# A two-layer diffusion trunk on one core: the FFN's closing norm and residual move into the FFN's program, and the modulation weights are loaded ahead of x

## What is computed

```
mod = split(silu(c) @ ada_w[layer] + ada_b[layer], 6)            # for the latent tokens; c_ctx for the context
h   = rms_norm(x, norm_pre_mix) * (1 + mod[1]) + mod[0]          # then four groups of mixing heads, and w_out
x   = x + mod[2] * rms_norm(o, norm_post_mix)
f   = conv_ffn(rms_norm(x, norm_pre_ffn) * (1 + mod[4]) + mod[3], w_up, conv, w_down)
x   = x + mod[5] * rms_norm(f, norm_post_ffn)                    # the closing norm and residual
rms_norm(v, g) = v * rsqrt(mean(v * v over the 1024 features) + 1e-6) * g
```

## Time and profile before

| What | us |
|---|---|
| median of three runs (4760.15 to 4768.19) | 4762.68 |
| the profiled execution's own time | 4763.57 |
| its span, first to last instruction | 4760.6 |
| TensorE busy in the span | 3919.5 (82%) |
| VectorE / ScalarE / GpSimd busy | 2133.6 / 1343.8 / 1150.1 |
| mean granted TensorE clock, share of full | 0.907 |

### The profile page before, as it was taken

One profiled execution on the slowest core, in us unless ns is written; L12 is line 12 of the kernel. 1 busy time (PEld: TensorE's weight loads), 2 busy tenths in 40 slices (PEclk: granted clock), 3 DMA queues, 4 the chain that ended last, 5 costly groups with the idle time before them and its releaser, 6 DMA issues. The chain is left out here.

```text
span 4760.6 us, 81723 instructions
## 1 busy us (share of the span) xinstructions
PE 3919.5 (82%) x33438; PEld 3150.5 (66%) x33438; DVE 2133.6 (45%) x2920; ACT 1343.8 (28%) x1879; POOL 1150.1 (24%) x884
## 2 busy tenths in 40 slices
PE   5999559576878999999993999559658888999995
PEld 2888435364767788888882787435437767888884
DVE  3444735465556432332236323735465555332234
ACT  4111333234333321211213211333243334222221
POOL 1000520203531232332321000520205512333322
PEclk8999669797988999999996999669779989999997
DMA  4444110101012111101101234110110021111112
GB/s 164 161 158 157 46 61 0 39 3 35 4 53 85 54 36 38 39 31 40 40 27 62 105 128 142 42 58 1 39 36 4 4 101 59 49 49 44 48 49 88
DMA packets 71558, 283.24 MB, mean 59 GB/s; under 512 B 7392, under 2 KB 12768, under 8 KB 66272
## 3 DMA queue, kind: packets, MB, share of 16 engines
q1 hardware_dynamic: 55136, 198.51, 12.2%
q10 hardware_dynamic: 16128, 80.49, 4.6%
HBM read 223.65 MB, written 47.45 MB: 57 GB/s over the span
## 5 line engine op out<-in xcount | busy, mean ns | idle before, releaser
L3444 DVE SCALAR_TENSOR_TENSOR y<-ps,taps,y 128x1023 f32<-128x1023 f32 (+1 forms) x132 | 134.2, 1016 | 866.2 <-DVEq L3442 859.7
L491 PE MATMUL ps<-h_hi,wu_hi 128*128 128x512 f32 x1680 | 460.4, 372 | 12.3 <-PEq L3344 12.3
L491 PE MATMUL ps<-h_hi,wu_raw_rest 128*128 128x512 f32 x1680 | 459.4, 371 | 0.0
L491 PE MATMUL ps<-h_whole_rest,wu_hi 128*128 128x512 f32 x1680 | 459.0, 371 | 0.0
L3489 POOL TENSOR_TENSOR wu_raw_rest<-wu_raw,wu_hi 128x1024 fp32r<-128x1024 f32 x84 | 201.3, 2397 | 1025.8 <-POOLq L3488 1025.8
L491 PE MATMUL ps<-h_hi,w_hi 128*128 128x512 f32 (+1 forms) x1200 | 314.9, 367 | 39.6 <-PEq L487 39.6
L491 PEld LDWEIGHTS ps<-h_hi,wu_hi 128*128 128x128 f32 x1680 | 294.6, 188 | 69.6 <-issue 13.5
L491 PEld LDWEIGHTS ps<-h_hi,wu_raw_rest 128*128 128x128 f32 x1680 | 294.6, 188 | 56.3
L491 PEld LDWEIGHTS ps<-h_whole_rest,wu_hi 128*128 128x128 f32 x1680 | 294.1, 188 | 56.2
L491 PE MATMUL ps<-h_hi,w_raw_rest 128*128 128x512 f32 (+1 forms) x1200 | 313.1, 365 | 0.0
L491 PE MATMUL ps<-h_whole_rest,w_hi 128*128 128x512 f32 (+1 forms) x1200 | 313.0, 365 | 0.0
(11 more groups left out here) (390 smaller groups left out, 8141.4 us busy)
## 6 DMA issues: line engine op xcount, KB each, us to landing
wu_raw<-in_w_up_dram SPq DMA_DIRECT2D x88, 512.0 KB, 3.3
w_raw<-in_w_in_dram SPq DMA_DIRECT2D x54, 512.0 KB, 4.6
ada_w<-in_ada_rest_dram ACTq DMA_DIRECT2D x27, 1024.0 KB, 6.8
rows<-rows ACTq DMA_DIRECT2D x42, 640.0 KB, 4.9
wd_raw<-in_w_down_dram SPq DMA_DIRECT2D x40, 512.0 KB, 4.2
h_whole<-rows SPq DMA_DIRECT2D x24, 640.0 KB, 6.3
ada_w<-in_ada_rest_dram ACTq DMA_DIRECT2D x27, 512.0 KB, 4.8
raw<-rows SPq DMA_DIRECT2D x20, 640.0 KB, 4.7
```

What stands on the lines that cost most here:

```text
L491: mm = pe.matmul(ps[:, lo:lo + width], w[a][:, t, :], rhs[b][:, t, lo:lo + width], start=(t == 0 and i == 0), stop=(t == n_k - 1 and i == 2))
L3444: dve.scalar_tensor_tensor(y[:, s, lo + 1:hi], ps[s][:, lo:hi - 1], k.taps[:, s, 0:1], y[:, s, lo + 1:hi], ALU.mult, ALU.add).then_inc(own ...
```

## The change

It has three places.

1. **Start.** `load_phase` loads only tiles 0 and 1 of x. The other six are issued by SyncE in the next block, behind its four tiles of modulation weights and ahead of the projection weights. TensorE multiplies seven tiles of modulation weights ahead of the ones product, and one after. VectorE's `between()` (the rests of the two projection weights) comes ahead of its wait for the turned sums.
2. **Closing inside the FFN's program, both layers.** `residual_phase` is gone. The spilled x comes back tile by tile into `k.h`, behind the last down weights. In the last group ScalarE squares each output tile when it is complete and multiplies it in place by its modulation (ACT.Identity with a scale), and VectorE adds the squares into `facc` between its additions. One ones product of `facc` and Ln and Exp follow. VectorE then multiplies each tile by the factor and adds x; the x of tiles 1, 3 and 5 is added by GpSimd.
3. **What follows a closed tile.** In layer 0 ScalarE squares it, TensorE sums it over features at once (ones products accumulated over the eight tiles), and the factor of layer 1's first norm is ready at the block's end in `k.factor`; layer 1's `Norm` begins with `between()` and the scaling. In layer 1 each closed tile is stored by a DMA of its own, and `store_phase` is gone.

The core of the diff:

```diff
@@ load_phase, Norm.sync
-                for t in range(KD):
+                for t in range(2):
                     sp.dma_start(k.xT[:, t, :], a["xT"][:, t, :]).then_inc(k.x_tiles[t].sem, 16)
...
             self.load_ada(sp, 0)
+            for t in range(2, KD):
+                sp.dma_start(self.k.xT[:, t, :], self.x[:, t, :]).then_inc(self.k.x_tiles[t].sem, 16)
@@ Norm.scalar, Norm.vector: squares, sum and factor only `if self.ada is not None`; in vector also
+        between()
         if self.ada is not None:
             dve.wait_ge(self.turned.sem, self.turned.at(1))
...
-        between()
-        dve.wait_ge(self.root_dve, 1)
-        dve.sem_inc(self.root_dve, -1)
+            dve.wait_ge(self.root_dve, 1)
+            dve.sem_inc(self.root_dve, -1)
@@ Norm.tensor
-            self.ada_products(pe, 0, KD // 2)
+            self.ada_products(pe, 0, KD - 1)
...
-            self.ada_products(pe, KD // 2, KD)
+            self.ada_products(pe, KD - 1, KD)
@@ input_projection_phase
-                norm.tensor(pe)
+                if layer == 0:
+                    norm.tensor(pe)
@@ mix_out_ffn_phase, SyncE behind load_last_down(sp)
+        def close_layer(sp):
+            for t in tiles:
+                sp.dma_start(k.h[:, t, 0:n], k.x_dram[:, t, 0:n]).then_inc(x_back.sem, 16)
+            if layer == DEPTH - 1:
+                for t in tiles:
+                    wait_closed(sp, t)
+                    sp.dma_start(a["out"][:, t, :], k.xT[:, t, 0:SEQ]).then_inc(stored.sem, 16)
+                sp.wait_ge(stored.sem, stored.at(16 * KD))
@@ VectorE: in vector_down's last group behind the addition of tile o: add_square(dve, o - 1)
+        def add_square(dve, o):
+            if o < 1:
+                return
+            dve.wait_ge(fsq_done.sem, fsq_done.at(o + 1))
+            if o > 1:
+                dve.wait_ge(facc_done.sem, facc_done.at(o - 1))
+            dve.tensor_tensor(facc, facc, y[:, o % 2, 0:n], ALU.add).then_inc(facc_done.sem, 1)
+        by_pool = (1, 3, 5)
+        def close_rows(dve):
+            dve.wait_ge(froot_done.sem, froot_done.at(1))
+            dve.wait_ge(x_back.sem, x_back.at(16 * KD))
+            for t in tiles:
+                dve.wait_ge(fmod_done.sem, fmod_done.at(t + 1))
+                dve.tensor_tensor(f[:, t, 0:n], f[:, t, 0:n], froot, ALU.mult).then_inc(fscaled.sem, 1)
+                if t:
+                    close_tile(dve, t - 1)
+            close_tile(dve, KD - 1)
+        def close_tile(dve, t):            # GpSimd has the same for the tiles of by_pool
+            if t in by_pool:
+                return
+            dve.wait_ge(fscaled.sem, fscaled.at(t + 1))
+            dve.tensor_tensor(f[:, t, 0:n], k.h[:, t, 0:n], f[:, t, 0:n], ALU.add).then_inc(x_closed.sem, 1)
@@ TensorE behind the last tensor_down
+                pe.wait_ge(facc_done.sem, facc_done.at(KD - 1))
+                for lo, w in SEGS:
+                    if lo < n:
+                        mm = pe.matmul(ps[0][:, lo:lo + w], k.const(C_ONES), facc[:, lo:lo + w], start=True, stop=True)
+                mm.then_inc(fsum_done.sem, 1)
+                if layer < DEPTH - 1:
+                    pe.wait_ge(f_done.sem, f_done.at(KD))
+                    for t in tiles:
+                        pe.wait_ge(xsq_done.sem, xsq_done.at(t + 1))
+                        for lo, w in SEGS:
+                            mm = pe.matmul(ps[1][:, lo:lo + w], k.const(C_ONES), y[:, t % 2, lo:lo + w],
+                                           start=(t == 0), stop=(t == KD - 1))
+                        mm.then_inc(xpart_done.sem, 1)
@@ ScalarE behind the last round_down
+                for o in tiles:
+                    act.wait_ge(f_done.sem, f_done.at(o + 1))
+                    if o > 2:
+                        act.wait_ge(facc_done.sem, facc_done.at(o - 2))
+                    act.activation(y[:, o % 2, 0:n] if o else facc, f[:, o, 0:n], ACT.Square).then_inc(fsq_done.sem, 1)
+                    act.wait_ge(fsq_done.sem, fsq_done.at(o + 1))
+                    for lo, hi, c in token_parts(n):
+                        ins = act.activation(f[:, o, lo:hi], f[:, o, lo:hi], ACT.Identity, scale=k.mods[:, 5 * KD + o, c:c + 1])
+                    ins.then_inc(fmod_done.sem, 1)
+                act.preload_act_table_set("natural_log_exp_and_others")
...             # wait for fsum_done, Ln and Exp into froot
+                if layer < DEPTH - 1:
+                    for t in tiles:
+                        wait_closed(act, t)
+                        if t > 1:
+                            act.wait_ge(xpart_done.sem, xpart_done.at(t - 1))
+                        act.activation(y[:, t % 2, 0:n], f[:, t, 0:n], ACT.Square).then_inc(xsq_done.sem, 1)
...                 # wait for xpart_done, Ln and Exp into factor, wait for its end
```

## The result

The changed kernel takes 4705.66 us in the median of four executions (4705.06 to 4706.04), the kernel before beside it 4765.18 (4760.15 to 4768.19): a ratio of 0.9876, with a 95% interval of 0.9859 to 0.9893. The forecast was 4698.0, with a range from 4686 to 4714. A later pair of the same two kernels on one chip gave 0.986 (0.9844 to 0.9876): 4705.49 against 4769.95.

The account below looks back on a forecast made before the run. TensorE, busy in 82% of the span, bounds the kernel, so time could come only from its idle stretches: 17.3 + 27.2 + 19.9 = 64.4 us off the profiled 4763.57 gives 4699.2, 4698 as median; range 4686 to 4714.

Parts of the forecast that it names:

- The chains of waits: Engine-to-engine waits at the start, between the layers and at the end; shortening them was to save 64.4 us.
- rivals 1, 2 and 4: Start bound elsewhere (0.12), TensorE cold in the closing (0.13), stores by tile bringing nothing (0.02); they help set 4714.
- the largest uncovered assumption: Loops between the three places run the same TensorE instructions, only shifted, and were costed at nothing.
- Start, 17.3 forecast: From the start to the first scaling of h: 53.1 instead of 70.38 us, 17.3 less.
- rival 1: Start bound elsewhere: uneven queues, long fixed part or clock falling ahead of the eighth tile; 4703 to 4705, chance 0.12.
- TensorE is nearly continuous there: At the start, the reason for forecasting 17.3 us, between 12 to 14 with a lowered clock and 18 without a pause.
- Between the layers, 27.2 forecast: From the FFN's last addition to layer 1's first scaling: 81.0 to 53.8 us, bounds on the gain 19 and 35.
- Rival 2: TensorE, idle before the closing, runs its ones products at the slow clock; about 4707, chance 0.13.
- The prediction's sign for this rival: Between the layers, ones products of 4.1 us at 2540 to 2570 would show TensorE cold in the closing.
- The end, 19.9 forecast: From layer 1's last FFN addition to the span's end: 56.9 to 37.0 us, bounds on the gain 16 and 27.
- the rule on the ports: In the closing, a two-SBUF-input VectorE operation is shut out for a whole GpSimd instruction; up to 7.2 us at the end.
- rival 5: Slower: the granted clock falls in the unchanged loops once rests between them are shorter; 4772 or more, chance 0.03.

Follow-up runs that it names:

- the run with eight tiles first: The changed kernel with all eight modulation-weight tiles multiplied ahead of the ones product and ScalarE's copies ahead of Ln and Exp; 4700.28 us, ratio 0.9852.
- the change again: The changed kernel run a second time, only blank lines added at the file's end; 4705.49 us against 4769.95, ratio 0.986.
- without GpSimd: The changed kernel with all eight closing additions on VectorE, none on GpSimd; median 4701.5 us, ratio 0.9854.
- one store: The changed kernel with the result stored in one 4 MB DMA behind the last closed tile, not eight; 4707.34 us in one execution.
- shifts: The changed kernel with 128, 64 or 192 more semaphore instructions on TensorE at the start of layer 1's input projection; medians 4705.66, 4707.47 and 4706.07 us.
- the repetition: The kernel before and the changed kernel both run again, only blank lines added; 4769.95 and 4705.49 us, ratio 0.986.

## Why the prediction was right, and where it was off

The chains of waits were right in all three places, and their sum was 65.8 where 64.4 stood. That the sum is so near is in part luck: the places were off by -3.1, +1.0 and +3.5 us, and these nearly cancel. The median came out 7.7 us above the forecast, within the range, but for a reason that the range was not made for: its upper end was rivals 1, 2 and 4, and what moved the time was an untouched stretch that the prediction cost at nothing, called there "the largest uncovered assumption". Term by term:

**Start, 17.3 forecast, 14.2 measured.** Three steps shifted. TensorE's seven tiles were done at 39.07, not 41.2, since the first tile landed at 12.9 and not at 14.6 and the seven took 26.2 and not 26.6. VectorE's chain of additions ended at 43.69, not 42.7: its first late addition came at 33.08, not 32.0. By the prediction's own rate the first late tile of x lands at 30.6 (29.1 and 1.5 for its 640 KB); ScalarE's square of it starts at 31.66. So the pause ahead of the ones product was 4.92 instead of 1.5, and the prediction's own warning came true: "the 1.5 us pause ahead of the ones product sends the clock down". From the end of the additions to the eighth tile it took 4.31 instead of 2.35: 1.66 for the clock (4.08 - 2.42) and 0.30 from VectorE's end to TensorE's start, which the forecast left out. 1.0 + 1.96 of the 3.1 lost are these; the remaining steps (eighth tile 3.6, copies and turning 3.5, bias and gain 1.1) were 0.2 above their rows. So the clock part of rival 1 did come, with a price of 1.7 us and not the whole 5 to 7 of that rival. The reasoning "TensorE is nearly continuous there" looked at a pause made of two forecast times, 41.2 and 42.7, off by 2.1 and 1.0 us in opposite directions. That the pause costs the clock is shown by the run with eight tiles first.

**Between the layers, 27.2 forecast, 28.2 measured.** The sum of the steps was 52.8 and the stretch is 52.8; the 1 us added on top for ones products at the slow clock was not needed. Last squares 3.51 (forecast 3.5), to the first use of the factor 7.01 (7.55), closing 26.4 (26.1), two products with Ln, Exp and the block's end 7.75 (7.8), the projection weights' load, rounding and rests 8.1 (7.8). Rival 2 (TensorE is cold in the closing) falls as a cost: of the eight products only the first ran wholly at the slow clock, beginning 8.44 us after TensorE's last, and that was off the path, since TensorE had caught up by 2533.62 and VectorE's closing went on to 2545.06. The prediction's sign for this rival, a ones product of 4.1 us there, did show for that one product; by itself it told nothing of the cost.

**The end, 19.9 forecast, 23.4 measured.** Last squares 3.0 instead of 4.2 (VectorE's pace in the last group is 2.78 a tile against the 2.9 assumed and TensorE's 2.72, so it hardly fell behind), factor 6.1 instead of 6.7, closing 21.3 instead of 20.8, last store 3.15 instead of 5.3. The last is the mis-sized term: the row taken for it, 4.6 us, is a median over stores of the same size from SBUF to device memory (ScalarE's queue, L582 of the kernel before), most of which share the DMA engines with other transfers. The trace of the kernel before shows one of these stores among others, and one that has the engines to itself. Windows 2850 to 2856 and 2969 to 2973 of its DMA view (all packets of the window, then the store):

```profile
DMA packets 432, 1.57 MB, mean 262 GB/s; under 512 B 48, under 2 KB 48, under 8 KB 432
...
rows<-rows ACTq DMA_DIRECT2D x1, 512.0 KB, 4.4
```

```profile
DMA packets 144, 0.52 MB, mean 131 GB/s; under 512 B 16, under 2 KB 16, under 8 KB 144
...
rows<-rows ACTq DMA_DIRECT2D x1, 512.0 KB, 2.6
```

The second is what the last store of the change measured, 2.6, and it could have been read ahead of the forecast. The Trainium skill (DMA: Bandwidth & Descriptors, Anatomy of one DMA) gives 2.0 us and the bytes, an estimate of 3.2. The page states that fit for DMAs that GpSimd issues, and these stores are SyncE's; the measurement was nearer to it than the row taken, and decides.

**GpSimd, 2.0 and 2.5 us each forecast, 2.13 and 2.69 measured.** Also right, behind the rule on the ports, that all additions on VectorE would be cheaper: 3.5 us between the layers and 2.8 at the end.

**The loops, 0 forecast, 9.2 us longer in the net, as much as the scan of layer 1 alone.** Not rival 5: that had the clock falling, and the scan's clock is 0.96 in all four profiles. What is shown is that the unchanged kernel's scan differs by 5.7 us between two profiled executions, and that the profile of before was at the low end. On one chip, three kernels whose scan is the same code (the change again, without GpSimd, one store) had 246.0, 248.0 and 243.1. Over all profiles the scan of layer 1 took 239.2, 244.7 and 245.0 in code that is as before around it, and 242.5 to 251.4 (242.5, 243.0, 243.1, 246.0, 248.0, 248.4, 251.4) in code as in the change without shifts; the scan of layer 0 took 250.6 to 255.6 with no side to it, and the other untouched stretches together 4306.6 to 4317.0. The means in layer 1, 243.0 and 246.1, are 3 us apart with three runs on one side. Whether a part of that belongs to the change is left open; so is what makes a scan long. Compared by the repetition, the three places give 13.9 + 28.0 + 23.1 = 65.0 us and the medians 64.5; in the first pair the medians are 59.5 apart. The forecast's 64.4 is the worth of the three places. The time that it was taken from, 4762.68 in the median, was low beside the 4767.14 and 4769.95 of the same kernel later.

## What to carry to other kernels

Before an idle engine is given part of a busy one's element-wise work, look in the trace for one pair of overlapping VectorE and GpSimd operations: where one of them ends its own duration behind the other, they take turns, and the split costs more than it saves. Where a forecast rests on a short pause between two estimated times, give the pause the errors of both, and if a pause can send the clock down, put the work that is left ahead of it. And take each stretch of a profile as one draw: here an untouched stretch of 240 us differed by 5.7 between two executions of the same kernel, and a repetition of before and after settles more than an explanation of one pair. When a row is taken as the price of a transfer, look at what else the DMA moved beside it.

## What the runs showed of the hardware

- TensorE's ones product of six instructions took 2.42 us with TensorE busy right ahead of it and 2.39 after 1.79 us of idle time, both at a granted clock of 1.00; it took 3.64 after 4.42 (clock 0.64), 4.08 after 4.92 (0.58) and 4.26 after 5.20 (0.56). The short pause cost only itself; each of the long ones also cost 1.2 to 1.8 us in the product behind it.
- GpSimd's addition of 128 x 1024 lasts 3.23 us in the closing and 4.0 to 4.1 at 128 x 1280; its subtraction alone takes 2.40 at 1024. The meeting lengthens both engines' operations: VectorE's multiplication from 1.2 to 3.35 us, GpSimd's addition by about the 0.9 that VectorE's addition beside it had still to run.
- Eight stores of 512 KB one after the other, each issued as its tile closes, cost 3.15 us behind the last tile; one store of 4 MB costs 12.2. A store of 512 KB lands in 2.6 us when the DMA moves nothing else, and in 4.4 with another 1 MB beside it.
- A scan of 7165 matmuls, at a granted clock of 0.95 to 0.97 and with the same instructions, took from 239.2 to 251.4 us in single executions.
